# Segment sums ahead of the masks in a chunked state-space scan on VectorE

## The reference

```python
acs = jnp.cumsum(dtc * a.reshape(SSD_GROUPS, r), axis=2)
lower = (pos[:, None] >= pos[None, :])[None, None, :, :, None, None]
seg = acs[:, :, :, None] - acs[:, :, None, :]
decay = jnp.exp(jnp.where(lower, seg, -jnp.inf))
cb = jnp.einsum('bcign,bcjgn->bcijg', cc, bc)
wts = cb[..., None] * decay * dtc[:, :, None]
y_diag = jnp.einsum('bcijgr,bcjgrp->bcigrp', wts, xc)
...
y_off = jnp.einsum('bcign,bcgrpn->bcigrp', cc, h_prev) * jnp.exp(acs)[..., None]
```

## Time and profile before

| what | value |
|---|---|
| median of three runs | 2168.02 us (2165.43 to 2169.4) |
| profiled execution, its own time | 2167.93 us |
| span of the profiled execution | 2166.2 us |
| PE busy | 2010.2 us, 93% |
| DVE busy | 1279.4 us, 59% |
| ACT busy | 999.7 us, 46% |
| POOL busy | 747.4 us, 35% |
| mean granted clock of TensorE | 0.965 |
| the scan | about 642 to 780 us |

### The profile page before, as it was taken

One profiled execution on the slowest core, in us unless ns is written; L12 is line 12 of the kernel. 1 busy time (PEld: TensorE's weight loads), 2 busy tenths in 40 slices (PEclk: granted clock), 3 DMA queues, 4 the chain that ended last, 5 costly groups with the idle time before them and its releaser, 6 DMA issues.

```text
span 2166.2 us, 30854 instructions
## 1 busy us (share of the span) xinstructions
PE 2010.2 (93%) x11973; PEld 1810.5 (84%) x11973; DVE 1279.4 (59%) x1911; ACT 999.7 (46%) x1771; POOL 747.4 (35%) x568
## 2 busy tenths in 40 slices
PE   4789999999998878999999998899999979899998
PEld 1579998799988866799987997699988767799986
DVE  0567761566527856677724795577741686677732
ACT  1244442454546634544424686544432535544432
POOL 0033234333346645333243840332333330333342
PEclk7889999999999999999999999999999989899999
DMA  9954337433420134644365510654456422244442
GB/s 370 385 214 127 122 111 251 169 120 119 126 83 21 40 122 145 255 145 127 117 228 180 197 60 0 253 185 122 122 179 210 156 102 89 80 139 125 126 126 78
DMA packets 77073, 320.98 MB, mean 148 GB/s; under 512 B 8672, under 2 KB 14208, under 8 KB 63104
## 3 DMA queue, kind: packets, MB, share of 16 engines
q1 hardware_dynamic: 76048, 318.18, 42.5%
q10 hardware_dynamic: 880, 0.82, 0.1%
HBM read 314.96 MB, written 4.01 MB: 147 GB/s over the span
## 4 chain that ended last, share of the span: by engine, by line
PE 80%; DVE 6%; ACT 4%; issue 3%; DMA 3%; POOL 3%; SPq 1%; DVEq 0%; ACTq 0%; POOLq 0%
PE pair L1670 17%; PE pair L1672 16%; PE pair L1671 16%; PE pair L1704 6%; PE pair L1705 6%; PE pair L1706 6%; PE pair L1810 2%; DVE x L1242 1%; DMA mod_more<-in_w_mod 1%; PE pair L1897 1%; PE pair L1898 1%; PE pair L1896 1%; POOL w_lo L675 1%; PE pair L1843 1%; DMA raw<-in_pool 1%
## 5 line engine op out<-in xcount | busy, mean ns | idle before, releaser
L675 POOL TENSOR_TENSOR w_lo<-raw,w_hi 128x512 fp32r<-128x512 f32 (+1 forms) x375 | 578.4, 1544 | 1198.7 <-ACT w_hi L817 1198.7
L1670 PE MATMUL pair<-h_hi,w_hi 128*128 128x386 f32 (+1 forms) x2008 | 689.0, 343 | 18.5 <-POOL h_lo L682 15.5
L1672 PE MATMUL pair<-h_hi,w_lo 128*128 128x386 f32 (+1 forms) x2008 | 684.4, 341 | 0.0
L1671 PE MATMUL pair<-h_lo,w_hi 128*128 128x386 f32 (+1 forms) x2008 | 683.7, 340 | 0.0
L1175 DVE TENSOR_TENSOR w_lo<-raw,w_hi 128x512 fp32r<-128x512 f32 x351 | 426.4, 1217 | 331.2 <-ACT w_hi L817 331.1
L817 ACT ACTIVATE w_hi<-raw 128x1024 fp32r<-128x1024 f32 x375 | 393.0, 1050 | 280.4 <-PE pair L1706 222.3
L1670 PEld LDWEIGHTS pair<-h_hi,w_hi 128*128 128x128 f32 (+1 forms) x2008 | 381.7, 190 | 23.2 <-POOL h_lo L682 21.8
L1671 PEld LDWEIGHTS pair<-h_lo,w_hi 128*128 128x128 f32 (+1 forms) x2008 | 382.4, 190 | 0.9
L1672 PEld LDWEIGHTS pair<-h_hi,w_lo 128*128 128x128 f32 (+1 forms) x2008 | 381.5, 190 | 0.3
L1299 DVE SCALAR_TENSOR_TENSOR acc<-pair,taps,acc 128x385 f32<-128x385 f32 x176 | 108.9, 619 | 214.2 <-ACT acc L904 214.2
L904 ACT ACTIVATE acc<-pair,taps 128x386 f32<-128x386 f32 x176 | 117.3, 667 | 237.8 <-PE pair L1672 237.8
(11 more groups left out here) (257 smaller groups left out, 2545.9 us busy)
## 6 DMA issues: line engine op xcount, KB each, us to landing
raw<-in_ffn_in SPq DMA_DIRECT2D x176, 512.0 KB, 3.5
raw<-in_ffn_out SPq DMA_DIRECT2D x88, 512.0 KB, 3.6
mod_raw<-in_w_mod SPq DMA_DIRECT2D x32, 1024.0 KB, 7.8
mod_base<-in_w_mod SPq DMA_DIRECT2D x31, 1024.0 KB, 7.5
mod_more<-in_w_mod SPq DMA_DIRECT2D x20, 1024.0 KB, 13.2
raw<-in_ssd_conv SPq DMA_DIRECT2D x32, 512.0 KB, 3.5
gb<-rows_dram SPq DMA_DIRECT2D x8, 1024.0 KB, 5.5
raw<-in_ssd_z SPq DMA_DIRECT2D x16, 512.0 KB, 3.5
```

What stands on the lines that cost most here:

```text
L675: pool.tensor_tensor(w_lo[:, m % SLOTS, 0:w], raw[:, m % SLOTS, 0:w], w_hi[:, m % SLOTS, 0:w].bitcast(F32), ALU.subtract).then_inc(w_low_p ...
L1670: ten.matmul(to, wh, h_hi[:, k, cols], start=k == 0, stop=False, skip_group_check=True)
L1671: ten.matmul(to, wh, h_lo[:, k, cols], start=False, stop=False, skip_group_check=True)
L1672: ins = ten.matmul(to, wl, h_hi[:, k, cols], start=False, stop=k == KD - 1, skip_group_check=True)
```

## The change

In `scan_dve` the masks go from the place in front of the segment sums to the place behind them, and the two operations of 128x128 become one of 128x256, whose first input (the product of C and B) is read twice by a broadcast. The wait for `s_copied` and the one for `s_w` go with them, and L1441 now waits for the last operation of the chain. No other engine's program changes.

```diff
                     if u:
                         take_state(*ALL_STEPS[u - 1][:3])
-                    vec.wait_ge(s_copied, u + 1)
-                    if u:
-                        vec.wait_ge(s_w, 2 * u)
-                    for d in range(2):
-                        ch.did(vec.tensor_tensor(cb_mask[:, d, :], turned[:, u % 2, P + GW:], tri[:, d, :], ALU.mult))
-                    masks = ch.n
                     if u >= SCAN_SLOTS:
                         vec.wait_ge(s_y, u - SCAN_SLOTS + 1)
                     vec.wait_ge(s_cum, 2 * u + 1)
...
                             ins.then_inc(s_seg, 1)
                         else:
                             ch.did(ins)
-                    ch.wait(masks)
+                    vec.wait_ge(s_copied, u + 1)
+                    if u:
+                        vec.wait_ge(s_w, 2 * u)
+                    ch.did(vec.tensor_tensor(cb_mask, turned[:, u % 2, P + GW:].unsqueeze(1).broadcast_to([P, 2, P]),
+                                             tri[:, :, :], ALU.mult))
+                    ch.wait()
                     for d in range(2):
                         vec.wait_ge(s_exp, 2 * u + d + 1)
```

## The result

| | median, us | lowest to highest |
|---|---|---|
| before, 10 runs | 2167.71 | 2165.13 to 2169.4 |
| with the change, 10 runs | 2173.18 | 2168.87 to 2175.01 |

The ratio is 1.0019, 95% interval 1.0011 to 1.0027: slower by about 4 us by the ratio and 5.5 by the medians. The forecast was "within 0.2%", at 2168.5 us. The direction is clear of zero, the size is at the edge of what had been called no change, and the median lies 0.8 us above the top of the range; by the ratio (1.0019 times 2168.02 is 2172.1) the time lies inside it. The profiled execution took 2174.18 us with a span of 2172.4, 6.2 more than before.

The account below looks back on a forecast made before the run. PE's waits in the scan were taken to hang on POOL's second L731 and ACT's L969, not on DVE's masks. 8 x 0.05 + 4 x 0.04 + 0 = +0.56 us on 2167.93 gave 2168.5 us, range 2164.5 to 2172.4.

Parts of the forecast that it names:

- The masks have a twin on ACT: Last steps: ACT's L969 ends 0.02 us from the segment sums, so L978 wins only 0.02 to 0.2 us.
- POOL's second L731 sets the weights: Last steps: L1441 waits for POOL's second L731, which the merged mask delays; +0.19 - 0.13 = +0.05 us a group.
- The 0.16 more for the middle steps: Middle steps with odd g: POOL's pair and L1441 0.04 us late, added in four groups (4 x 0.04).
- First and middle steps: First steps: sums 0.83 us earlier, turned into idle time before L1399, gain 0; middle steps: sums no earlier.
- The first group: First group of heads: PE's 2.4 us of waits for the sums nearly go, but L1412 holds PE; 0, within -2.4 and 0.
- the slower rival: Last steps: mask falls behind both L731, +0.35 us each, +0.41 more with even g; 4.4 us, 2172.4 us; 6%.
- The sum for the scan: Whole scan: terms of last steps, middle steps and first group together, +0.56 us.
- The clock: TensorE's granted clock: waits that change places can bring or remove a fall to 1.2 GHz; +-1.5 us, in the range.

Follow-up runs that it names:

- The run from PSUM: Against the changed kernel: the merged mask reads the product of C and B from PSUM, not its SBUF copy; median 2169.76 us, ratio 1.0031.
- the control: The kernel before, unchanged, run again with a second profile; median 2167.62 us, ratio 1.0.
- the order alone: Against the changed kernel: masks stay behind the sums but are two operations of 128x128 again; median 2177.61 us, ratio 1.0046 to the kernel before.

## Why the prediction was right, and where it was wrong

**The masks have a twin on ACT: right.** L978 starts right behind L969 in last steps, and earlier by 0.20 only.

**POOL's second L731 sets the weights: right, with its size.** The forecast worked out 1.27 + 0.19 for the second L731: measured 1.46. It had the merged mask 0.28 behind the first L731: 0.28. It had +0.05 us for each wait of PE: measured +0.05 and +0.04 in the seven groups behind the first. The 0.16 more for the middle steps does not show: these seven groups cost 0.34 us in sum. The run from PSUM shows the cause by taking it away.

**First and middle steps: right.** The 0.8 us of the first step turned into idle time before L1399. In last steps the sums came 0.65 us earlier and not 0.8: the forecast had counted the wait for ACT's L963 in middle steps only. This had no effect, since L978 waited for L969.

**The first group: wrong in size.** The term was 0, within -2.4 and 0, and it is +0.42, up to the end of PE's wait in that group. The exponentials of its steps come earlier, as was said, but POOL's L715 then gets in front of the second weights operation with g = 0 too (L1440 1.47 and 1.09 us there), which was priced for the slower rival at +0.41 and had not been asked of this group. The lower bound had been thought of, the upper had not.

**The sum for the scan:** +0.56 forecast, +0.76 measured (0.42 + 0.34). That the two are so near is in part luck: the first group was 0.4 too low, and the others 0.2 too high.

**The clock: the step that failed.** The forecast had one fall more or less, +-1.5 us, "in the range", and took it as noise around the sum. In place of this term stand 1.2 + 1.1 us around the scan's end, which a delay of 1 us reproduces, and 2.5 to 3 us in the attention stage, 1000 us behind the change. The first part can come or go between executions of one kernel (the control has it too), but the medians go with it; the second is in all kernels but the kernel before, its control and the order alone. Both have the same sign here. This is why the measured 5.5 us by the medians is ten times the sum. The forecast of no change held because 0.19% lies just inside 0.2%, not because this term was seen.

**The slower rival** had the right side and nearly the right time, 2172.4 us, for a reason that is not there: the mask does get its turn between the two L731. Where the masks are two, the rival's mechanism is the one that the run of the order alone shows.

## What to carry to other kernels

Where the chain of waits names an operation, look for another engine that ends at the same time, and for what holds the next operation's data (here POOL at the port), before any of its time is counted as gain. Compare a change with the same kernel under a delay of its size, and with one that has the same number of instructions: in a kernel tuned to a fraction of a percent, both alone were worth more (3 and 7 us, of which the 3 are a part) than the edit's 0.76 us in the scan. The mask with one input in PSUM did not queue with GpSimd (0.417 us at most).

## What the runs showed of the hardware

- A mask or weights operation of VectorE with two SBUF inputs that met a running GpSimd instruction in the scan ended 0.14 to 0.15 us (128 elements, 25 cases before), 0.28 (256, 16 cases with the change) or 0.55 to 0.56 (512, 32 cases in both) behind it. Between two GpSimd instructions that follow each other without a gap one waiting VectorE operation is served; of two masks the second waited for the whole next GpSimd instruction (2.28 us for the pair).
- With one input in PSUM the same 128x256 operation took 0.411 to 0.417 us in all 24 steps beside a busy GpSimd.
- 1 us of idle time in a kernel of 2168 us cost 7 us by the medians, 3.4 us cost 6.5. Some 3 us of both are in the attention stage, where a delay is not needed; the rest follows where the falls of TensorE's granted clock lie (3.4 or 6.8 us long behind the scan).
- A stall of 0.2 to 0.4 us behind a wait stands at every 128th recorded instruction of VectorE's stream where it can be seen (18 of 18 in 14 traces), and goes when instructions ahead of it are added or taken away; in the attention stage three kernels have it and eleven do not, and these are 2.4 to 3.2 us longer there.
